# Retention squares summed on VectorE, and a split lookahead of zero while modulation weights pass the ring

## The reference

```python
mu = jnp.mean(of, axis=-1, keepdims=True)          # of: (tokens, 4 heads, 512)
var = jnp.mean(jnp.square(of - mu), axis=-1, keepdims=True)
on = ((of - mu) * lax.rsqrt(var + GN_EPS)).reshape(B, L, H * DV) * gn_g
return (jax.nn.silu(gate) * on) @ w_o
```

## Time and profile before

| | |
|---|---|
| median of three runs | 1450.25 us (1447.91 to 1450.72) |
| the profiled execution | 1449.64 us, span 1447.9 us |
| PE busy | 1381.7 us, 95% of the span |
| DVE, ACT busy | 767.1 us, 611.1 us |
| granted clock of PE, mean | 0.973 of full |
| retention heads | about 21 to 214 us of the span |
| modulation groups 4 to 7 | about 603 to 632 us |
| experts | from about 1190 us |

### The profile page before, as it was taken

How to read it: one execution, slowest core, us unless ns; L and a number is a source line. 1 busy time by engine, 2 the same in 40 slices (tenths; PEclk the granted TensorE clock), 3 DMA queues, 4 the chain that set the end, 5 groups by cost and what they waited for, 6 DMA issues and landing times.

```text
span 1447.9 us, 25571 instructions
## 1 busy us (share of the span) xinstructions
PE 1381.7 (95%) x9884; PEld 1189.3 (82%) x9884; DVE 767.1 (53%) x1338; ACT 611.1 (42%) x1016; POOL 10.6 (1%) x23
## 2 busy tenths in 40 slices
PE   6999999999999999989999999999999789999995
PEld 5899989899999798678999989889999755555543
DVE  6456646655554776346666556758546542222213
ACT  4544554533333564345444444656534321121122
POOL 0000020000000000000000000000000000000000
PEclk9999999999999899999999998999999889999999
DMA  9654345655555544367555563332134559999970
GB/s 361 127 180 146 132 161 175 242 173 173 174 174 178 215 143 132 126 239 245 190 181 186 188 235 130 131 114 76 59 102 146 199 205 409 408 405 405 406 306 29
DMA packets 80293, 289.78 MB, mean 200 GB/s; under 512 B 9536, under 2 KB 10560, under 8 KB 80064
## 3 DMA queue, kind: packets, MB, share of 16 engines
q1 hardware_dynamic: 78480, 284.65, 55.1%
q0 software_dynamic: 1712, 3.68, 1.7%
HBM read 285.14 MB, written 3.15 MB: 199 GB/s over the span
## 4 chain that ended last, share of the span: by engine, by line
PE 85%; DVE 8%; ACT 3%; issue 2%; DMA 1%; SPq 0%; DVEq 0%; ACTq 0%
PE bank L746 18%; PE bank L750 17%; PE bank L749 17%; PE bank L1364 12%; PE bank L901 2%; ACT w_hi L1440 1%; DVE ring_low L1872 1%; PE bank L1349 1%; PE bank L1325 1%; PE bank L1326 1%; PE bank L781 1%; PE bank L1350 1%; DMA ring<-weights 1%; PE bank L823 1%; DVE rstd L1904 1%
## 5 line engine op out<-in xcount | busy, mean ns | idle before, releaser
L1872 DVE TENSOR_TENSOR ring_low<-ring,w_hi 128x1024 fp32r<-128x1024 f32 x292 | 356.3, 1224 | 290.2 <-ACT w_hi L1440 287.8
L746 PE MATMUL bank<-hn_hi,w_hi 128*128 128x272 f32 (+1 forms) x1456 | 425.1, 292 | 6.1 <-DVE hn_low L1891 3.9
L750 PE MATMUL bank<-hn_hi,ring_low 128*128 128x272 f32 (+1 forms) x1456 | 418.1, 287 | 0.0
L749 PE MATMUL bank<-hn_low,w_hi 128*128 128x272 f32 (+1 forms) x1456 | 417.6, 287 | 0.0
L1440 ACT ACTIVATE w_hi<-ring 128x1024 fp32r<-128x1024 f32 x292 | 307.1, 1054 | 207.5 <-PE bank L746 174.4
L746 PEld LDWEIGHTS bank<-hn_hi,w_hi 128*128 128x128 f32 x1456 | 277.3, 190 | 12.8 <-DVE hn_low L1891 6.4
L750 PEld LDWEIGHTS bank<-hn_hi,ring_low 128*128 128x128 f32 x1456 | 277.9, 191 | 0.0
L749 PEld LDWEIGHTS bank<-hn_low,w_hi 128*128 128x128 f32 x1456 | 277.5, 191 | 0.2
L746 PE MATMUL bank<-arena_r,w_hi 128*128 128x256 f32 (+1 forms) x848 | 246.7, 291 | 9.1 <-DVE arena_r L2392 3.6
L750 PE MATMUL bank<-arena_r,ring_low 128*128 128x256 f32 (+1 forms) x848 | 243.6, 287 | 0.0
L749 PE MATMUL bank<-arena_r,w_hi 128*128 128x272 f32 (+1 forms) x784 | 225.3, 287 | 0.0
(11 more groups left out here) (386 smaller groups left out, 1620.8 us busy)
## 6 DMA issues: line engine op xcount, KB each, us to landing
ring<-weights SPq DMA_DIRECT2D x436, 512.0 KB, 4.3
tab<-weights SPq DMA_DIRECT2D x32, 512.0 KB, 6.7
w_late<-weights SPq DMA_DIRECT2D x32, 512.0 KB, 8.1
arena<-weights SPq DMA_DIRECT2D x32, 512.0 KB, 5.9
tab<-tables SPq DMA_DIRECT2D x1, 2857.0 KB, 17.6
skew<-arena POOLq DMA_DIRECT2D x1, 2048.0 KB, 46.5
h<-tokens SPq DMA_DIRECT2D x2, 544.0 KB, 4.1
tab<-skew POOLq DMA_DIRECT2D x8, 128.0 KB, 3.5
```

The costliest lines, as they stand in the source:

```text
L746: begun = mm(dst[:, 0:cols], wh, high(k), start=k == 0, stop=False)
L749: mm(dst[:, 0:cols], wh, low(k), start=False, stop=False)
L750: last = mm(dst[:, 0:cols], wl, high(k), start=False, stop=k == K - 1)
L1872: tt_(ring_lo[:, slot, :], ring[:, slot, :], w_hi[:, n % SPLITS, :], ALU.subtract).then_inc(S("w_lo_ready"), 1)
```

## The change

In retention, DVE adds all of `sq[1]`, `sq[2]` and `sq[3]` to `sq[0]`, before and not after the splits of gate tile 2. PE sums `sq[0]` alone, by one matmul, in gate tile 3 after the tile's blocks 0 and 1. Counts of `sq_added` are adapted. In MLA, `splits_for` adds 0 for tiles from `sum4` to before `sum7`, 1 for `sum7` and 2 from there to wo1; before it added 2 up to and with `sum7`, then 3. In `kn1` to `sum4` it stays 2.

```diff
             last = tile_unit[t] if t >= 0 else -1
             need = sum(u <= last for u in dense_units)
-            inside = at["kn", 1] <= t < at["am", MH - 1]
-            most = need + (AHEAD - 1 if t in before_norm or inside else AHEAD)
+            ahead = AHEAD
+            if t in before_norm or at["kn", 1] <= t < at["sum", 4] or t > at["sum", MH - 1] and t < at["wo1"]:
+                ahead = AHEAD - 1
+            elif at["sum", 4] <= t <= at["sum", MH - 1]:
+                ahead = 1 if t == at["sum", MH - 1] else 0
+            most = need + ahead
...
-        a = 2 * RH
+        a = 3 * RH
...
             def ret_gate(hh, first):
-                for t in range(first, first + 2):
-                    if t == 3:
+                def variance(k):
+                    if k == 2:
                         if hh:
                             pe.wait_ge(S("gn_root"), hh)
-                        wait_stored(pe, at["av", hh] + 3)
-                        pe.wait_ge(S("sq_added"), 2 * hh + 2)
-                        mm(bank[7][:, 0:T0], ones, sq[:, 3, :], start=True, stop=False)
-                        mm(bank[7][:, 0:T0], ones, sq[:, 0, :], start=False, stop=True).then_inc(S("gn_var"), 1)
-                    dense(DT, x_hi, x_lo, T0)
+                        pe.wait_ge(S("sq_added"), 3 * hh + 3)
+                        mm(bank[7][:, 0:T0], ones, sq[:, 0, :], start=True, stop=True).then_inc(S("gn_var"), 1)
+
+                for t in range(first, first + 2):
+                    dense(DT, x_hi, x_lo, T0, variance if t == 3 else None)
...
-                lows(gate_tile(hh, 2))
                 wait_stored(dve, at["av", hh])
-                for d in range(1, 3):
+                for d in range(1, 4):
                     wait_stored(dve, at["av", hh] + d)
                     add_square(sq, d, 0, T0)
+                lows(gate_tile(hh, 2))
                 dve.wait_ge(S("gn_root"), hh + 1)
```

## The result

| | before, beside it | changed |
|---|---|---|
| median of four runs | 1449.08 us (1445.77 to 1450.72) | 1432.75 us (1430.84 to 1434.31) |
| ratio, 95% interval | | 0.9891 [0.9873, 0.9909], about 15.8 us |
| the profiled execution | 1449.64 us, span 1447.9 | 1431.61 us, span 1429.8 |
| mean granted clock | 0.973 | 0.976 |

The page has PE at the same work in a shorter span; eight records fewer are the four sums that are gone.

What follows compares the result with a forecast made beforehand. PE, busy for 95% of the span, was taken to bound the kernel. Retention 5.4 + MLA 8.2 = 13.6 us off 1449.64 gave 1436.0, or 1436.6 as median; own bounds 1433.5 to 1438, range with (a) and (b) 1433.5 to 1441.5.

Steps and rivals of the forecast that it cites:

- the root follows its table load: Retention, ACT: root can start at 65.89, when its table load ends, so the chain comes forward by 0.42 us only.
- the 0.61 that was taken: Retention, PE: cost in us of one fp32 sum inside gate tile 3, giving a gain of 1.50 a head.
- the bounds: Retention, PE: one sum costs between 0.41 and 0.99 us; gain of a head 1.1 to 1.7.
- the wait at block 12: wo0 after the last retention head: PE waits 0.62 us, once, for DVE's low part.
- The term 8.2: MLA, from `sum5` to wo1: gain in us from removing PE's wait before `join5` and the low clock behind it.
- Upper: 8.17: MLA: upper bound in us of the gain, 5.85 of stall and another 2.32 of low clock; the lower bound was nothing.
- the low end: Whole kernel: 1433.5 us, with the sum at 0.41, no wait at block 12 and a run at the spread's low end.
- (a): MLA to wo1: short lookahead or low clock takes back a part; 1438.9 for either, 1441.2 for both; chance 0.20.
- (b): Retention: adds come as late as now and the sum waits inside the tile; 1.6 in place of 5.4, 1440.4; chance 0.07.
- (c): MLA: the wait moves to `join6`, `join7` or wo1, so only retention's 5.4 stays; 1444.8; chance 0.06.
- (d): wo1: PE starved of splits, up to 18.3 us for eight units, so slower at 1454.9; chance 0.03.
- Wo1 about 13.6 us earlier: Sign in the profile after: wo1 starts about 13.6 us earlier than 632.63, or 8.2 counted from `sum5`.

Runs made afterwards that it cites:

- w0_early: Changed kernel with lookahead 1 instead of 0 in sum 4 to sum 6, so w0 alone is split ahead of the copy of sum 5; ratio 0.9936.
- ret_only: Changed kernel with the old `splits_for`, so only the retention part against the kernel before; ratio 0.9954 (6.7 us).
- sum_between: Changed kernel with its one sum of squares between gate tiles 2 and 3 instead of inside tile 3, adds still early; ratio 0.9909.
- late_adds: Changed kernel with the three adds of squares back behind the split of gate tile 2, the one sum still in tile 3; ratio 0.9939.
- before_reach: Kernel before, with no split 11 or more units past the previous tile's last, from wo0 and from wo1 through the following modulation groups; ratio 1.0105.

## Why the prediction was right, and where it was wrong

**Retention.** Right in each step. The adds are hidden, no sum waits, and the root follows its table load. One sum costs less than the 0.61 that was taken: matmul by matmul in the first pair of traces, PE's lead grew by 1.65, 1.64, 1.63 and 1.63 us in the four heads, so a sum costs 2.11 - 1.63 = 0.48 (0.46 in head 0), inside the bounds. With it the wait at block 12 is larger by the same 0.13: 0.74 us for 0.62. Counted by starts, block 12 comes 0.9 us behind its turn, and its second matmul another 0.1 (212.23 - 212.00 = 0.23 in place of 0.13). Sum: 4 x 1.63 - 0.9 = 5.6 for 5.4; the three traces give 5.5. Where the prediction weighed the Trainium skill (ScalarE: Activation LUTs, What ACT_TABLE_LOAD costs), that section counts about 1.38 us of drain to each table load, which was to hold the root. The row above has the root 0.01 us behind the load's end, so no such drain shows here.

**MLA.** The mechanism is right: ACT stood before a load that nobody needed yet, and `w0_early` brings the stall back with one unit. Without the stall the clock stayed at full, and w0 and w1 cost nothing. The size was read from a single execution, the mildest of four with the stall in them: the stretch took 24.14, 25.72, 25.13 and (`ret_only`) 26.08 us, and 15.88 without it. The term 8.2 is that first trace's (24.14 - 15.88 = 8.3); the mean of the three of before is 9.1. "Upper: 8.17" was no bound. In the table the surplus of 0.9 is balanced by the second row, because the two traces of before with a larger loss here took 2.6 us less in the stretch ahead. That may be chance: `ret_only` took 390.08 us there, like the changed kernel, and still 26.08 here.

**The failed step is the sum, and the low end set on it.** It held the two edits and took all the rest of the kernel as unchanged, for no reason given. That put at nothing 1.7 us (0.6 + 1.1) behind wo1 and behind the second down projection: the loads there landed late in five of six cases before and in none of six after. The waits stood in the profile of before, as PE waits on squares of 2.6 us in two (1.6 of them behind wo1) and 1.2 in one, and I had not asked what decides them. 13.6 + 1.7 = 15.3 is what the traces show (15.4); the runs have 15.8 by the ratio. The other part of the miss is the base: the runs of before had a median of 1449.08 beside the changed kernel, 1.2 below the 1450.25 from which I counted. With both, the forecast would have been 1436.6 - 1.7 - 1.2 = 1433.7, and the 0.9 left to 1432.75 is less than the interval. The low end was added up wrongly too: its three parts (0.8 us for the sums, 0.62 for block 12, 2.34 for a run of 1447.91 in place of 1450.25) lead from 1436.6 to 1432.8, not 1433.5.

Is the 1.7 us the work of the change? For the 0.6 behind wo1 nothing speaks for it: the kernel before showed both landings there, and so did `sum_between`, so the three early ones of the changed kernel are best put down to luck. For the 1.1 behind the second down projection it is open. Its early landing came in all three traces of the changed kernel and in none of the three of before, but it lasts over dozens of loads at a time, and `sum_between`, one moved sum away, had them mostly early in one trace and all late in the other.

**The rivals.** (a) did not come: the clock was 1.00 and wo1 waited for no split. (b) is what `late_adds` shows, 2.1 us for its 1.6. (c) did not come: no join waited over 0.3 us. (d) did not come in the changed kernel, but its mechanism is real: `before_reach` paid 18.5 us in waits for low parts when the lookahead was cut over two whole phases.

**The marks.** "Wo1 about 13.6 us earlier" was 15.4 in this trace: 7.1 had been won by `join4` (609.54 - 602.40), 5.65 of it by retention, 0.7 at the very start (PE's first sums follow each other by 0.45 us until 10.5 us in the trace of before, until 9.2 in this one, and by 0.23 after that) and 0.8 in the stretch between, where the clock was low for 13.7 us before and for 10.2 after; from there to wo1 it was 8.2, as forecast. The 0.7 and the 0.8 lie where the edits do nothing, so most of the 1.8 us above the mark is no work of the change.

## What to carry to other kernels

On an engine that works strictly in order, ask of every piece of work done ahead what stands behind it, and whether its load can have landed by then; but cut it only there, since a cut in all tiles of two phases made the kernel 15 us slower. Size a stall with the clock that it costs from several executions, and read the spread of the stretches that the change does not touch as well, because they move the result by as much as a small edit. Put an add early where its engine is idle before you look for a cheaper place for its consumer.

## What was not expected of the hardware

- At the two places behind wo1 and the second down projection, a 512 KB load in 16 parts had two landing times, 3.1 to 3.5 and 4.1 to 4.4 us, in all 18 traces. In the late case one to three of the parts came 0.8 to 1.1 us after the others. Early or late could last over 60 loads in a row.
- One stall of 5.2 to 6.6 us on PE came with 6.8 us of low clock in one execution and 10.2 in three others (in one of these a part of it fell ahead of the stall).
- One fp32 sum among dense matmuls costs 0.46 to 0.48 us, between tiles as within.
